# Sums of squares for three RMS norms: added tile by tile on VectorE, one multiplication with the ones matrix at the end of the stage

## What is computed

```python
def rmsnorm(x, g):
    y = xf * lax.rsqrt(jnp.mean(xf * xf, axis=-1, keepdims=True) + EPS)
    return (y * g.astype(jnp.float32)).astype(x.dtype)

def swiglu_half(x, g_pre, w_gate, w_up, w_down, g_post):
    h = rmsnorm(x, g_pre)
    y = (jax.nn.silu(h @ w_gate) * (h @ w_up)) @ w_down
    return x + 0.5 * rmsnorm(y, g_post)
...
    y = (jax.nn.sigmoid(gate_a) * y_a + jax.nn.sigmoid(gate_b) * y_g) @ w_out
    x = x + rmsnorm(y, g_post)
```

## Time and profile before

| what | value |
| --- | --- |
| median of 3 runs | 1577.23 us (1574.39 to 1577.93) |
| the profiled execution | 1584.02 us |
| its span, first to last instruction | 1581.7 us |
| TensorE busy | 1502.9 us, 95% |
| VectorE busy | 625.8 us, 40% |
| ScalarE busy | 501.5 us, 32% |
| GpSimd busy | 224.6 us, 14% |
| granted TensorE clock, mean | 0.981 of full |

### The profile page before, as it was taken

The page is one execution under the profiler, slowest core; times in us unless marked ns, Lnnn a source line. Parts: engine busy times, 40 slices in busy tenths (PEclk is TensorE's granted clock), DMA queues, the critical chain, the costliest instruction groups (busy, mean ns, idle before and its releaser), DMA issues. The chain is left out here.

```text
span 1581.7 us, 31163 instructions
## 1 busy us (share of the span) xinstructions
PE 1502.9 (95%) x12556; PEld 1379.6 (87%) x12556; DVE 625.8 (40%) x927; ACT 501.5 (32%) x742; POOL 224.6 (14%) x204
## 2 busy tenths in 40 slices
PE   7999999999798999999998999969979999999995
PEld 7999999999587878877876877759979999999995
DVE  5434333221633664123366543446254434332223
ACT  5322223121521355222134323243344222222221
POOL 0111111000152000323200320011031111110000
PEclk9999999999899999999999999989989999999998
DMA  4222223221359996999997567926202222223221
GB/s 152 93 93 93 92 85 109 92 91 64 115 165 389 344 307 235 373 336 333 381 316 265 180 225 261 313 73 223 84 36 94 93 93 93 87 92 109 89 76 54
DMA packets 111939, 268.77 MB, mean 170 GB/s; under 512 B 15401, under 2 KB 15914, under 8 KB 111090
## 3 DMA queue, kind: packets, MB, share of 16 engines
q1 hardware_dynamic: 105586, 244.25, 44.8%
q0 software_dynamic: 6272, 23.34, 4.1%
HBM read 253.29 MB, written 14.26 MB: 169 GB/s over the span
## 5 line engine op out<-in xcount | busy, mean ns | idle before, releaser
L131 DVE TENSOR_TENSOR w_low<-w_raw,w_high 128x1024 fp32r<-128x1024 f32 (+1 forms) x180 | 233.2, 1297 | 643.2 <-ACT w_high L127 628.8
L127 ACT ACTIVATE w_high<-w_raw 128x1024 fp32r<-128x1024 f32 (+1 forms) x180 | 200.6, 1116 | 729.0 <-PE psum L152 690.7
L148 PE MATMUL psum<-h_high,w_high 128*128 128x260 f32 x1344 | 270.6, 282 | 1.7 <-DVE w_low L131 1.7
L152 PE MATMUL psum<-h_high,w_low 128*128 128x260 f32 x1344 | 270.9, 283 | 0.0
L150 PE MATMUL psum<-h_low,w_high 128*128 128x260 f32 x1344 | 270.4, 283 | 0.0
L148 PEld LDWEIGHTS psum<-h_high,w_high 128*128 128x128 f32 x1344 | 207.2, 188 | 2.4 <-DVE w_low L131 2.4
L152 PEld LDWEIGHTS psum<-h_high,w_low 128*128 128x128 f32 x1344 | 207.2, 188 | 0.0
L150 PEld LDWEIGHTS psum<-h_low,w_high 128*128 128x128 f32 x1344 | 206.6, 188 | 0.0
L148 PE MATMUL psum<-mix_h_high,w_high 128*128 128x260 f32 x704 | 148.1, 292 | 6.7 <-DVE mix_h_low L296 6.1
L148 PE MATMUL psum<-a_high,w_high 128*128 128x260 f32 x704 | 144.2, 286 | 0.0
L150 PE MATMUL psum<-mix_h_low,w_high 128*128 128x260 f32 x704 | 143.3, 285 | 0.9 <-issue 0.9
(11 more groups left out here) (325 smaller groups left out, 1913.9 us busy)
## 6 DMA issues: line engine op xcount, KB each, us to landing
kv_ring<-in_cache_k SPq DMA_DIRECT2D x256, 256.0 KB
kv_ring<-in_cache_v SPq DMA_DIRECT2D x256, 256.0 KB
w_raw<-in_w_gu SPq DMA_DIRECT2D x88, 512.0 KB
w_raw<-in_w_dn SPq DMA_DIRECT2D x32, 704.0 KB
w_raw<-in_w_proj SPq DMA_DIRECT2D x44, 512.0 KB
spill<-h_f POOLq DMA_DIRECT2D x20, 260.0 KB
gates<-spill POOLq DMA_DIRECT2D x16, 260.0 KB, 3.6
w_raw<-in_w_merge SPq DMA_DIRECT2D x8, 512.0 KB
```

The costliest lines, as they stand in the source:

```text
L127: act.activation(w_high[:, u, 0:nk, :], w_raw[:, u, 0:nk, :], ACT.Copy).then_inc(high_done, 1)
L131: dve.tensor_tensor(w_low[:, u, 0:nk, :], w_raw[:, u, 0:nk, :], w_high[:, u, 0:nk, :].bitcast(F32), ALU.subtract).then_inc(low_done, 1)
L148: pe.matmul(out[h], w_high[:, u, k, :], high[:, k0 + j, tok[h]], start=s, stop=False)
L152: mm = pe.matmul(out[h], w_low[:, u, k, :], high[:, k0 + j, tok[h]], start=False, stop=e)
```

## The change

VectorE clears `h_f[:, 0, :]` ahead of each of the three stages, and adds the squares of tiles 0 to 6 to it as they come. TensorE no longer multiplies tile by tile: at the end of the stage it multiplies the ones matrix with `h_f[:, 0, :]`, and then with the squares of tile 7, into the same banks. The count that `norm_sum` reaches stays 8, with 7 counted by VectorE and the last by TensorE.

```diff
+        def squares_cleared(dve, n):
+
+            dve.memset(h_f[:, 0, :], 0.0).then_inc(squares_zero, 1)
+            dve.wait_ge(squares_zero, n // 2 + 1)
+
+        def squares_added(dve, k, n, u):
+
+            dve.wait_ge(norm_sq, k + (n * KD + 1))
+            dve.wait_ge(norm_sum, k + n * KD)
+            dve.tensor_tensor(h_f[:, 0, :], h_f[:, 0, :], sq[:, u, :], ALU.add).then_inc(norm_sum, 1)
+
+        def squares_total(pe, n):
+
+            pe.wait_ge(norm_sum, (n + 1) * KD - 1)
+            for h in range(2):
+                pe.matmul(psum[:, 6 + h, 0:HT], ones[:, :], h_f[:, 0, h * HT:(h + 1) * HT], start=True, stop=False)
+            square_sum(pe, KD - 1, n, 1, stop=True)
...
                             if not (tail and u == 1):
                                 split_low(dve, m * 2 + (nb + 2 * u + 2), 0, NKD)
                                 split_low(dve, m * 2 + (nb + 2 * u + 3), 1, NKD)
+                                squares_added(dve, m + u, norm_n + 1, u)
+                    squares_cleared(dve, norm_n + 1)
                     with dve.Fori(0, KD // 2 - 1) as i:
                         down(i * 2)
                     down(KD - 2, tail=True)
...
                             block_products(pe, m * 2 + (nb + 2 * u + 1), 1, range(NKD), u, a_high, a_low, NKD, False, True)
-                            if not (first and u == 0):
-                                square_sum(pe, m + (u - 1), norm_n + 1, 1 - u, start=first)
...
-                    square_sum(pe, KD - 1, norm_n + 1, 1, stop=True)
+                    squares_total(pe, norm_n + 1)
...
+                    squares_cleared(dve, norm_n)
                     for m in range(KD - 1):
                         split_low(dve, nb + 2 + m, m % 2, KD)
+                        squares_added(dve, m, norm_n, m % 2)
...
                         block_products(pe, nb + m, m % 2, range(KD), m % 2, mg_high, mg_low, 0, True, True,
                                        by_chunk=(m_low, 0) if m == 0 else None)
-                        if m:
-                            square_sum(pe, m - 1, norm_n, (m - 1) % 2, start=(m == 1))
-                    square_sum(pe, KD - 1, norm_n, 1, stop=True)
+                    squares_total(pe, norm_n)
```

More of the change, by code:

```diff
@@ L159, in program @@
         first_sum = sem("first_norm_sum")
+        squares_zero = sem("square_sums_cleared")
         norm_rec = sem("norm_factor")
```

## The result

The changed kernel takes 1559.84 us (median of 4 runs, 1559.24 to 1561.63), the kernel before beside it 1577.13 us: a ratio of 0.9898, 95% interval 0.9887 to 0.9910. The forecast was 1561.7 us, in a range of 1557.4 to 1566.5. In a later repetition the ratio was 0.9905 (0.9888 to 0.9921).

A forecast was written before the change was run, and what follows sets the result against it. TensorE, busy without a gap in the three stages, was taken as the bound. Removing 18 sums, 12 x 0.87 + 6 x 0.85 = 15.5 us, with all else at cost 0, gave 1577.23 - 15.5 = 1561.7 us, range 1557.4 to 1566.5.

The forecast's parts named there:

- The stages are TensorE's alone: Three stages: TensorE has no idle time, so products behind a removed sum move up by all of it; 15.5 us.
- The size of a sum: Time TensorE spends on one square sum, taken from tile periods: 0.87 us in down stages, 0.85 in merge.
- The chain's piece: In the last down stage's chain of work on TensorE, one square sum takes 0.88 us; upper bound of its cost.
- Six sums, the end unchanged: Each stage loses six of eight sums on TensorE, 18 in all; the stage's end stays as it was, cost 0.
- VectorE's adds and memset cost nothing: VectorE in the three stages: 21 adds of 0.70 us and a memset ahead of each stage fit idle time, cost 0.
- Rival 1: TensorE's removed sums give back only their weight loads, 0.66 us each: gain 11.9 us, 1565.3 us; chance 4%.
- Rival 2: Behind the first down projection a transfer sets the next start, losing 5.2 us: 1566.9 us; chance 6%.
- Rival 3: At the stage ends TensorE's clock falls to 1.2 GHz, doubling the last sums: 5.2 us back, about 1566.9; chance 2%.
- Rival 4: TensorE's next tile waits for high part, square and add in a row: 31 us more, 1608 us; chance 2%.
- Rival 5: VectorE's adds disturb TensorE's products by as much as they relieve them, 0.74 us each: time 1577; chance 2%.

The follow-up runs named there:

- e1: The changed kernel with merge given back its old sums, only the two down stages changed; 1573.57 us against 1584.41 for the kernel before, ratio 0.9933.
- e2: Only merge changed, the down stages keep their sums between the products; 1579.0 us, ratio 0.9966 to the kernel before.
- c1: The kernel before, with six sums in each stage taken over half of the columns; 1577.57 us against 1583.95, ratio 0.9962.
- e3: The changed kernel, with VectorE adding tile 7 too and TensorE multiplying once; ratio 0.9899 to the kernel before.
- h1: The changed kernel with filler memsets ahead of each add, two in down stages, one in merge; 1569.72 us beside 1583.95 for the kernel before.
- h4: The changed kernel with filler memsets ahead of each add, four in down stages, two in merge; 1567.19 us beside 1575.21 for the kernel before.
- e4: The changed kernel, with the second feed-forward block's opening norm also summed by VectorE and multiplied once; 1567.94 us, ratio 0.9896 to the kernel before.
- e6: The changed kernel, with GpSimd instead of VectorE clearing `h_f` and adding; 1559.65 us, ratio 0.9900 to the kernel before.

## Why the prediction was right

- *The stages are TensorE's alone, and a removed sum moves all behind it up.* Shown: e1 and e2 by stage, and the windows without idle time.
- *The size of a sum.* 5.32 / 6 = 0.887 in the down stages and 5.20 / 6 = 0.867 in merge, where 0.87 and 0.85 were taken; 15.8 us in all where 15.5 were forecast. The chain's piece of 0.88 us would have been the better pick. The medians gave 17.3 and 15.0 us, on either side of it, and the intervals of both ratios take 15.8 us in.
- *Six sums, the end unchanged.* Right, and c1 and e3 show both sides of it: what stands in the gap behind the last product is free, what stands behind ScalarE's last square is paid.
- *VectorE's adds and memset cost nothing.* Right: 0.69 us for an add as priced, 0.49 for a memset within its bounds. In the down stages 5.62 us of idle time are left where 5.5 were forecast, and h1 with 2.3 us more in merge is free too.
- *Rival 1, the weight loads as the price (0.66 us for a sum):* refuted by 0.88 for the whole and 0.44 for half the columns with all loads kept. The share of weight loads, was no price for an operation here. The Trainium skill (Perfetto Trace Analysis, "Identifying the Most-Contended Engine") puts it above the matmuls' busy time as a measure of how near a kernel is to its best; it states no price of an operation, so the runs don't contradict the page, only the rule that I had made of it.
- *Rival 2, absorbed behind a stage:* no. The mixer was as long behind a changed stage (e1) as behind an old one (e2).
- *Rival 3, the clock:* it didn't happen, the granted clock is 1.00 from 1136.57 to 1138.61, over the two last sums of merge, and over those of the last down stage. h4 has it at 0.52 there, behind a wait that the change doesn't have.
- *Rival 4, the add as the bound:* it didn't happen, but its stated threshold of 8.5 us in merge was wrong: h4 lost 7.1 us with 5.3 us of filler and add. I had added the idle time and the lead of one split, as if each tile began afresh. The cover is smaller, and in order: 2.5 us for the last add, then the period of the products for VectorE's whole work of a tile. I had the 2.4 us in the prediction, and didn't use them as the limit.
- *Rival 5, the adds disturb the products:* no, the periods are 15.84 us (1437.06 to 1452.90 between two splits of the last down stage) and 5.75, with the adds in them.

## What to carry to other kernels

A small reduction that sits between the products of a TensorE-bound stage costs its whole length each time; if another engine can fold the partial results first, the stage gets back that length for each but the ones that already lay in a gap. The cover on the other engine has two limits: its whole work for a tile must stay below the period, and before that is reached, the very last partial result has only the room until it is read. Where that engine is full already, as in e4, the same move gives nothing, however much it relieves TensorE.

## What the runs showed of the hardware

- VectorE and GpSimd shut each other out in the operations shown here, which all read two inputs from SBUF. In e4 VectorE's add took 1.80 us instead of 0.69 when it began inside one of GpSimd. In e6 VectorE began first and kept its 1.22 us, and GpSimd's add took 1.85 us, of which 0.68 lay before VectorE's end at 1111.84. By the Trainium skill (SBUF — State Buffer, "Who interferes with whom") a VectorE instruction with two inputs in SBUF contends with a GpSimd instruction that reads SBUF, and the order of issue decides which of them is blocked; the traces agree. Whether an operation with one input is spared was not tried.
- A plain F32 sum is priced by its columns down to 130 of them: 0.44 us for two matmuls, four weight loads included.
- After 5.5 us of waiting TensorE's granted clock was at 0.52, and the piece from the start of the two last sums to the root took 3.50 us instead of 2.04 (h4).
